# The expert stage's result stores issued by ScalarE instead of GpSimd

## The chip, the cores and the metric

The kernel runs on one core of one Trainium2 chip. The metric is the device time of one execution in microseconds (us), the median of several runs.

## The reference, cut to what matters

One inference step of a two-layer decoder for 256 prompt tokens and 8 x 4 sample tokens (288 in all, 1024 features). Each layer ends with a mixture of experts: a router picks two of 16 experts for each token, and the token's new value is a layer norm of ALPHA times its old value plus the weighted outputs of the two experts.

```python
h = jax.nn.silu(jnp.einsum('td,edf->tef', x, wg)) * jnp.einsum('td,edf->tef', x, wu)
h = h * combine[..., None].astype(h.dtype)
return jnp.einsum('tef,efd->td', h, wd)
...
xp = layer_norm(ALPHA * xp + moe(...), ln_g[l, 2], ln_b[l, 2])
```

`combine` is zero except for a token's two experts. All values are float32, and an expert has three matrices of 2 MB.

## The kernel before, in words

Attention, convolution, gating and cross-attention come first in each layer, and the change doesn't touch them. What matters is the expert stage, `experts(l)`, which runs once in each of the two layers.

**Work.** Only the tokens that chose an expert are computed for it. They are handled in chunks of at most 32 rows (CAP); an expert has one chunk, or more where it has over 32 tokens. A table of steps, computed on VectorE after the router, says which expert comes when and how many chunks it has; `last` is the number of the last chunk, read from memory by every engine. A chunk goes round the engines:

1. TensorE multiplies the chunk's rows with the gate and up matrices into `psS` (`gate_up`), and picks the rows of the next chunk into `psN` (`picked`).
2. ScalarE takes the silu of the gate half (`silu(c)`, L2158). In between it copies the next chunk's picked rows out of `psN` (`rows_in_order(c + 1)`, L2148), and after TensorE has turned them it copies them again (L2150).
3. VectorE multiplies silu and up (L1873), TensorE turns the product into `psV`, VectorE copies it (L1875) and makes the next table of rows (`table`), and TensorE multiplies with the down matrix into `psV`. Before it turns a product it waits until the last chunk's result has left `psV` (`S.y`).
4. VectorE copies the result into one half of `YS` (`rows_left`, L1881). `YS` has two halves, so chunk c waits there until the stores of chunks 0 to c - 2 have landed (`S.stored`, 64 for each chunk, from four DMAs of 16).
5. GpSimd stores the half to the HBM buffer `by_slot` with four DMAs of 32 rows x 1 KB (L2272). It waits until all earlier stores have landed before it issues the next four.

**Weights.** SyncE loads the weights of an expert with three DMAs (L682: gate and up, one run of 16 KB for each of 128 partitions; down, runs of 4 KB). There are three sets of buffers, so the load of expert step k + 3 is issued when TensorE signals that step k is done (`expert_used`). The three first experts are loaded ahead of the stage. After layer 0's experts SyncE goes on to the weights of layer 1 (L647, L658).

**End of the stage.** When the stores of all chunks but the last have landed, GpSimd gathers each token's result of the second pick (`gather(1, YB, ...)`, L2284, three indirect DMAs), then stores the last chunk, waits for it, and gathers the first pick (`gather(0, YA, ...)`). ScalarE meanwhile scales the tokens by ALPHA (L2165, L2166, `x_scaled`). VectorE adds the low pick to them (`z_low`, L1900), then the other one (`z_rows`, L1908), and takes the norm. In layer 0 TensorE then turns the rows back (L1277) and layer 1 begins; in layer 1 SyncE writes the outputs.

## Time and profile before

| | us |
|---|---|
| median of 3 runs | 1327.65 (1323.92 to 1329.11) |
| the profiled execution, its own time | 1324.23 |
| its span on the core | 1322.6 |

```profile
PE 1139.5 (86%) x10768; PEld 746.4 (56%) x10769; DVE 417.7 (32%) x1149; ACT 265.4 (20%) x541; POOL 226.4 (17%) x399
...
PE   6998788999999879998868999989998799988850
...
ACT  1013732112230321111101302111411411111101
POOL 2003995000000001322212100000000012222222
...
DMA  9746779943359729799999800715779197999972
```

The first line is each engine's busy time in the span, its share and its number of instructions. Below it the span is cut into 40 slices of 33 us; a digit is the busy share of a slice in tenths. PE is TensorE, DVE is VectorE, ACT is ScalarE, POOL is GpSimd, and DMA is the mean of the core's 16 DMA engines. Layer 0's expert stage lies in slices 15 to 22, layer 1's in the last nine. Of the page's other parts, the DMA queues are named by number: q1 is SyncE's, q10 ScalarE's (both hardware_dynamic), q0 GpSimd's (software_dynamic).

### The profile page before, as it was taken

Reading aid. Unit: us, or ns where it says so; the run is one execution under the profiler, and the core shown is the slowest. Engines: PE = TensorE matmul, PEld = TensorE weight load, DVE = VectorE, ACT = ScalarE, POOL = GpSimd, SP = SyncE. Lnnn points to the kernel's source line nnn. Section 1 sums busy time; section 2 is a strip of 40 time slices with the busy share of each in tenths; the row PEclk is TensorE's granted clock in tenths of the full one; section 3 lists DMA queues with packets and bytes.
Section 4 is the critical chain, followed back from the end, with each engine's and each line's share of the span. In section 5 each row is a group of like instructions: output and inputs, shape, how many; then the busy total and the mean of one; then the engine's idle time right before and its main releaser. Section 6 shows DMA issues by size and latency. Waiting matters only on the chain.

```text
span 1322.6 us, 27256 instructions
## 1 busy us (share of the span) xinstructions
PE 1139.5 (86%) x10768; PEld 746.4 (56%) x10769; DVE 417.7 (32%) x1149; ACT 265.4 (20%) x541; POOL 226.4 (17%) x399
## 2 busy tenths in 40 slices
PE   6998788999999879998868999989998799988850
PEld 4676545575776645554435776657765455555520
DVE  0026562713142452221112301522522622222216
ACT  1013732112230321111101302111411411111101
POOL 2003995000000001322212100000000012222222
PEclk9999997999999979998888999999999799999976
DMA  9746779943359729799999800715779197999972
GB/s 323 273 128 194 236 247 325 388 165 123 132 219 384 311 107 423 302 403 422 425 423 383 307 0 27 296 40 214 255 284 401 47 399 306 400 389 393 423 304 75
DMA packets 102625, 360.33 MB, mean 272 GB/s; under 512 B 9639, under 2 KB 11703, under 8 KB 94362
## 3 DMA queue, kind: packets, MB, share of 16 engines
q1 hardware_dynamic: 89986, 332.68, 65.7%
q0 software_dynamic: 12432, 26.51, 5.7%
q8 instruction: 42, 0.69, 0.2%
q10 hardware_dynamic: 144, 0.28, 0.1%
q14 instruction: 21, 0.17, 0.0%
HBM read 341.48 MB, written 18.38 MB: 272 GB/s over the span
## 4 chain that ended last, share of the span: by engine, by line
PE 58%; DMA 19%; DVE 10%; issue 7%; ACT 3%; SPq 1%; POOLq 1%; POOL 1%; DVEq 0%; ACTq 0%
PE acc L733 37%; DMA by_slot<-feats 10%; PE psS L733 8%; DMA ring<-in_w_exp_down 5%; PE psV L733 4%; PE psN L733 3%; DVE feats L1468 2%; DMA feats<-in_w_exp_down 2%; PE acc L1039 2%; PE acc L848 1%; DMA ring<-in_w_in_even 1%; DMA arena<-by_slot,arena 1%; PE psN L1157 1%; ACT arena L1346 1%; ACT feats L2148 1%
## 5 line engine op out<-in xcount | busy, mean ns | idle before, releaser
L733 PE MATMUL acc<-feats,ring 128*128 128x288 f32 x1280 | 315.7, 409 | 10.5 <-ACT feats L2057 4.2
L733 PEld LDWEIGHTS acc<-feats,ring 128*128 128x128 f32 x1280 | 244.7, 192 | 80.2 <-issue 9.5
L2272 POOL DMA_DIRECT2D by_slot<-feats x208 | 103.8, 499 | 524.6 <-DVE feats L1881 321.9
L733 PE MATMUL psS<-ring,feats 128*32 128x256 f32 x2176 | 138.8, 412 | 40.1 <-issue 38.8
L733 PEld LDWEIGHTS psS<-ring,feats 128*32 128x32 f32 x2176 | 74.8, 119 | 93.8 <-issue 56.0
L733 PE MATMUL psS<-arena,feats 128*32 128x256 f32 x1408 | 88.9, 402 | 22.6 <-issue 22.0
L2158 ACT ACTIVATE feats<-psS 64x256 f32<-64x256 f32 x52 | 19.6, 377 | 333.5 <-PE psS L733 333.5
L1346 ACT ACTIVATE arena<-acc 128x1024 f32<-128x1024 f32 (+6 forms) x86 | 65.4, 781 | 103.3 <-PE acc L733 34.7
L733 PE MATMUL psN<-arena,feats 128*32 128x256 f32 (+1 forms) x1360 | 83.5, 379 | 1.5 <-DVE feats L1800 1.5
L1873 DVE TENSOR_TENSOR feats<-feats,psS 64x256 f32<-64x256 f32 x52 | 22.1, 425 | 195.2 <-ACT feats L2158 194.3
L733 PEld LDWEIGHTS psS<-arena,feats 128*32 128x32 f32 x1408 | 45.7, 115 | 55.7 <-issue 31.7
L733 PE MATMUL psV<-ring,feats 128*32 128x256 f32 x1088 | 65.8, 382 | 0.8 <-DVE feats L1875 0.8
L1881 DVE COPY feats<-psV 128x256 f32 (+1 forms) x52 | 22.1, 425 | 134.9 <-DMA by_slot<-feats 95.8
L733 PEld LDWEIGHTS psN<-arena,feats 128*32 128x32 f32 x1360 | 44.1, 112 | 30.0 <-issue 3.2
L733 PE MATMUL acc<-arena,ring 128*128 128x256 f32 x256 | 58.4, 390 | 0.8 <-ACT arena L1346 0.8
L733 PE MATMUL acc<-ring,arena 128*128 128x512 f32 x128 | 56.9, 597 | 0.0
L1468 DVE SCALAR_TENSOR_TENSOR feats<-arena,cparT,feats 128x256 f32<-128x256 f32 (+1 forms) x180 | 55.9, 385 | 0.0
L733 PEld LDWEIGHTS acc<-arena,ring 128*128 128x128 f32 x256 | 49.8, 196 | 8.6 <-issue 1.5
L1628 DVE SCALAR_TENSOR_TENSOR feats<-feats,acc 128x288 f32<-128x288 f32 x32 | 14.5, 454 | 115.3 <-PE acc L733 115.3
L733 PE MATMUL acc<-arena 128*128 128x256 f32 (+6 forms) x174 | 35.5, 361 | 13.3 <-DVE arena L1434 5.7
L733 PEld LDWEIGHTS psV<-ring,feats 128*32 128x32 f32 x1088 | 31.9, 109 | 24.4 <-DVE feats L1875 6.9
L2051 ACT ACTIVATE feats<-feats 128x576 f32<-128x576 f32 x16 | 10.7, 683 | 151.5 <-DVE feats L1607 151.5
(344 smaller groups left out, 1224.3 us busy)
## 6 DMA issues: line engine op xcount, KB each, us to landing
ring<-in_w_exp_gate SPq DMA_DIRECT2D x22, 2048.0 KB, 15.1
ring<-in_w_exp_up SPq DMA_DIRECT2D x22, 2048.0 KB, 16.2
ring<-in_w_exp_down SPq DMA_DIRECT2D x22, 2048.0 KB, 24.2
arena<-in_w_exp_gate SPq DMA_DIRECT2D x10, 2048.0 KB, 15.1
arena<-in_w_exp_up SPq DMA_DIRECT2D x10, 2048.0 KB, 19.5
feats<-in_w_exp_down SPq DMA_DIRECT2D x10, 2048.0 KB, 23.8
ring<-in_cache_k SPq DMA_DIRECT2D x64, 256.0 KB, 3.2
ring<-in_cache_v SPq DMA_DIRECT2D x64, 256.0 KB, 3.1
```

Source lines behind the costliest of these rows:

```text
L733: return pe.matmul(out, lhsT, rhs, start=first, stop=last)
L848: last = pe.transpose(ACC("kt", 4 * i + b4)[:, 256 * f + P * t:256 * f + P * t + P], K[:, 2 * b4 + t, at:at + P], ident)
L1039: last = pe.transpose(ACC(f"xkt{l}", 4 * i + b4)[:, 256 * f + P * t:256 * f + P * t + P], K[:, b4, t, at:at + P], ident)
L1157: last = pe.transpose(psN[:, P * j:P * j + P], XR[:, P * j:P * j + P], ident)
L1346: return lambda out, in_: eng.activation(out, in_, ACT.Copy)
L1468: ins = dve.scalar_tensor_tensor(out=y, in0=u, scalar=tap, in1=y, op0=ALU.mult, op1=ALU.add)
L1628: dve.scalar_tensor_tensor(out=zT[:, i, :], in0=xT[:, i, :], scalar=ALPHA, in1=ACC(stage, i)[:, 0:NTOK], op0=ALU.mult, op1=ALU.add).then_i ...
L1873: dve.tensor_tensor(H[64:128, :], SG[64:128, :], psS[64:128, 0, 0:256], ALU.mult).then_inc(S.h, 1)
L1881: dve.tensor_copy(to, psV[:, 0:256]).then_inc(S.y, 1)
L2148: act.activation(XR, psN[:, 0:256], ACT.Copy).then_inc(S.rows_out, 1)
L2158: act.activation(SG[64:128, :], psS[0:64, 0, 0:256], ACT.Silu).then_inc(S.silu, 1)
L2272: pool.dma_start(by_slot[rows, 256 * q:256 * q + 256], YS[32 * q:32 * q + 32, at]).then_inc(S.stored, 16)
```

## The change

The four store DMAs of each chunk are issued by ScalarE. In its loop, pass c takes the silu of chunk c, copies the rows of chunk c + 1, waits until the stores of chunks 0 to c - 2 have landed, and then stores chunk c - 1. The last chunk is stored behind the loop, ahead of the scaling by ALPHA. GpSimd only gathers: the second pick once the stores of all chunks but the last have landed, the first pick once all have. The number and size of the DMAs, the two halves of `YS` and VectorE's waits stay as they are.

```diff
                 silu(0)
                 rows_in_order(1)
-                with act.Fori(1, last + 1) as c:
+
+                def store(c, rows, at):
+
+                    act.wait_ge(S.y, c + 2)
+                    for q in range(4):
+                        act.dma_start(by_slot[rows, 256 * q:256 * q + 256], YS[32 * q:32 * q + 32, at]).then_inc(S.stored, 16)
+
+                silu(1)
+                rows_in_order(2)
+                act.wait_ge(slots_zero, 16 * NXT)
+                store(0, slice(0, CAP), slice(0, 256))
+                with act.Fori(2, last + 1) as c:
                     silu(c)
                     rows_in_order(c + 1)
+                    act.wait_ge(S.stored, 64 * (c - 1))
+                    store(c - 1, slot_rows(c - 1), bass.ds(((c - 1) & 1) * 256, 256))
+                act.wait_ge(S.stored, 64 * last)
+                store(last, slot_rows(last), bass.ds((last & 1) * 256, 256))
...
                 last = pool.value_load(LASTI[0:1, 0:1], min_val=NE - 1, max_val=NCHUNK - 1)
-                def store(rows, at):
-
-                    for q in range(4):
-                        pool.dma_start(by_slot[rows, 256 * q:256 * q + 256], YS[32 * q:32 * q + 32, at]).then_inc(S.stored, 16)
-
-                pool.wait_ge(S.y, 2)
-                store(slice(0, CAP), slice(0, 256))
-                with pool.Fori(1, last) as c:
-                    pool.wait_ge(S.y, c + 2)
-                    pool.wait_ge(S.stored, 64 * c)
-                    store(slot_rows(c), bass.ds((c & 1) * 256, 256))
-
...
                 gather(1, YB, gathered_low)
-                pool.wait_ge(S.y, last + 2)
-                store(slot_rows(last), bass.ds((last & 1) * 256, 256))
```

## Rows read from the trace of the kernel before

**Rows 1.** Chain that ended last: start us, us, engine or DMA, what.

```profile
673.81 31.95 DMA ring<-in_w_exp_down
...
1227.92 6.92 DMA by_slot<-feats
...
1248.55 30.23 DMA ring<-in_w_exp_down
...
1294.69 1.71 DMA by_slot<-feats
...
1298.80 4.29 DMA arena<-by_slot,arena
```

**Rows 2.** Timeline of SyncE: start us, us, line, DMA issued.

```profile
577.86 0.34 SPq L682 DMA_DIRECT2D arena<-in_w_exp_gate  x1
...
1083.02 0.34 SPq L682 DMA_DIRECT2D arena<-in_w_exp_gate  x1
...
1213.87 0.35 SPq L682 DMA_DIRECT2D ring<-in_w_exp_gate  x1
```

**Rows 3.** Windows: length, busy by engine, PEclk, DMA share, GB/s.

```profile
1104.00:1114.00 10.00, 9.73 (x161) 5.55 (x160) 2.99 (x12) 1.65 (x5) 3.10 (x7) 1.00 0.31 113
...
1220.00:1240.00 20.00, 17.92 (x296) 10.25 (x298) 4.88 (x19) 2.90 (x8) 3.99 (x8) 1.00 1.02 428
```

**Rows 4.** Timeline of VectorE: start, us, instruction [idle before it <- what ended that].

```profile
1087.75 0.42 DVE L1873 TENSOR_TENSOR feats<-feats,psS 64x256 f32<-64x256 f32 x1 [4.21 <-ACT feats L2158]
...
1095.30 0.43 DVE L1873 TENSOR_TENSOR feats<-feats,psS 64x256 f32<-64x256 f32 x1 [3.16 <-ACT feats L2158]
...
1160.54 0.42 DVE L1873 TENSOR_TENSOR feats<-feats,psS 64x256 f32<-64x256 f32 x1 [1.50 <-ACT feats L2158]
...
1168.41 0.42 DVE L1881 COPY feats<-psV 128x256 f32 x1 [5.51 <-DMA by_slot<-feats]
1168.86 0.42 DVE L1873 TENSOR_TENSOR feats<-feats,psS 64x256 f32<-64x256 f32 x1
...
1218.96 0.42 DVE L1873 TENSOR_TENSOR feats<-feats,psS 64x256 f32<-64x256 f32 x1 [3.19 <-ACT feats L2158]
```

**Rows 5.** Timeline of ScalarE between two chunks of one expert.

```profile
1195.61 0.38 ACT L2150 ACTIVATE feats<-psN 128x256 f32<-128x256 f32 x1 [0.53 <-PE psN L1157]
1200.95 0.38 ACT L2158 ACTIVATE feats<-psS 64x256 f32<-64x256 f32 x1 [4.96 <-PE psS L733]
```

**Rows 6.** Timeline of GpSimd: the stores of two chunks.

```profile
1215.95 2.38 POOL L2272 DMA_DIRECT2D by_slot<-feats  x4 [3.05 <-DVE feats L1881]
1226.04 2.39 POOL L2272 DMA_DIRECT2D by_slot<-feats  x4 [7.71 <-DVE feats L1881]
```

**Rows 7.** DMA view of 1219.7 to 1225.0 us: packets by size, then by queue (packets, MB, share).

```profile
DMA packets 273, 2.24 MB, mean 424 GB/s; under 512 B 80, under 2 KB 80, under 8 KB 144
...
q0 software_dynamic: 128, 0.13, 7.0%
```

**Rows 8.** The same view of 701.9 to 703.9 us, SyncE's loads with 1 KB rows.

```profile
DMA packets 511, 0.74 MB, mean 369 GB/s; under 512 B 15, under 2 KB 436, under 8 KB 511
```

**Rows 9.** L2272, the DMA issued at 1217.8 us alone.

```profile
DMA to landing us min/median/max: 7.4/7.4/7.4
```

**Rows 10.** DMA issues on the two hardware queues: both at the start, then SyncE's L658 at 719.5.

```profile
L1957 ACTq DMA_DIRECT2D cst<-in_const x1: 435/435/435, 0.9 to 0.9; - x1
0.92 0.46 SPq L611 DMA_DIRECT2D arena<-in_x_prompt  x1
...
L658 SPq DMA_DIRECT2D ring<-in_w_in_odd x1: 5897/5897/5897, 719.5 to 719.5; - x1
```

**Rows 11.** Timeline at layer 1's end.

```profile
1289.61 1.90 ACT L2165 ACTIVATE arena<-arena 128x2048 f32<-128x2048 f32 x1
...
1292.48 5.67 DVE L1900 SCALAR_TENSOR_TENSOR arena<-arena 128x1024 f32<-128x1024 f32 x3 [0.56 <-ACT arena L2166]
...
1303.19 1.28 DVE L1908 SCALAR_TENSOR_TENSOR arena<-arena 128x1024 f32<-128x1024 f32 x1 [5.03 <-DMA arena<-by_slot,arena]
```

## The prediction

> **What bounds the kernel now.** I read the chain that ended last first. In both expert stages it ends in a long piece that is one load of down weights: 31.95 us in layer 0, landing at 705.8, and 30.23 us in layer 1, landing at 1278.8 [rows 1]. In layer 1 most of the chain ahead of it is a row of "DMA by_slot<-feats" pieces, the stores that this change moves; one stands for some 20 of them [rows 1]. Such a chain follows whatever was released last, even where it came last by 0.1 us, so it doesn't say what the stores cost. For that I went to two other views.
>
> First, SyncE's timeline against the windows. The load of step k + 3 is issued when step k is done. The issue at 1083.02 is the load behind step 2, the one at 1213.87 the load behind step 9 [rows 2]. Up to there the DMA engines run dry between loads: from 1104 to 1114 their share is 0.31 at 113 GB/s while PE is busy 9.73 of 10 us [rows 3]. So in that stretch the pace of the chunks decides when the next load starts. Behind 1213.87 four loads (steps 12 to 15) run without a gap, at share 1.02 and 428 GB/s [rows 3], until 1278.8: 64.9 us, 16.2 each, whatever the chunks do. **The end of layer 1's stage is therefore: time at which step 9 is done, plus four loads, plus one chunk and the tail.** In layer 0 the same point is the issue at 577.86, behind step 5 [rows 2], with eight loads to 705.8, 16.0 us each.
>
> Second, VectorE's timeline, for the pace. Within one expert two L1873 lie 7.55 us apart (1087.75, 1095.30); this is TensorE's own time for a chunk. Later in layer 1 VectorE waits for a landing 5.51 us before its result copy, and the next L1873 comes at 8.32 us instead (1160.54 to 1168.86) [rows 4]. From 1087.75 to 1218.96 there are 16 steps, 131.2 us, 9 of them within an expert [rows 4]. Four of the nine are late like the one shown (0.66 to 0.79 us, 2.9 together), and about 0.5 of that is made good at the change of expert behind them. So **all of the store waits cost about 2.4 us in layer 1's paced stretch**, and that is the whole prize. In layer 0's paced stretch I found no L1873 that was late.
>
> **Removed from GpSimd.** Its issues, 2.38 us for four [rows 6], were beside other work; removing their busy time (103.8 us on the page) is worth nothing by itself.
>
> **Added to ScalarE.** Four hardware-queue issues per chunk. ScalarE's only DMA took 0.435 us [rows 10], SyncE's with register addresses 0.34 [rows 2] and a move each; 4 x 0.45 = 1.8 us. They start when the rows of the next chunk are copied, and until the next silu ScalarE is idle 4.96 us within an expert [rows 5]. So the issue itself is hidden, with 3.2 us to spare; uncovered it would be 1.8 us x 52.
>
> **The wait that is new** is the one ahead of the issue: the stores of chunk c - 2 must have landed before ScalarE issues those of c - 1. What is queued behind it on ScalarE is silu(c + 1), and for that wait VectorE, then TensorE. Before, the same wait stood on GpSimd, behind which nothing else was queued. There a late store delayed only the result copy two chunks later, which can itself be 3 us late (TensorE needs the copy only when it turns the next product). Now the chain from store to store must fit in 7.55 us, or 10.7 once, with the 3.2 spare used up.
>
> **How long is that chain?** Under weight traffic GpSimd's was 10.1 us from store to store (1215.95 to 1226.04) [rows 6]. The DMA issued last, at 1217.8, took 7.4 us to land, at 1225.2 [rows 9]. The packets of this store lie in the window of 5.3 us: 128 of its queue, 8 on each of 16 engines, and 129 (273 less 144) weight packets of over 8 KB [rows 7]. So each engine took store and weight packets in turn, one for one, and a turn lasted 5.3 / 8 = 0.66 us. GpSimd's 8 packets per engine are 4 of data, two rows of 1 KB together (0.13 MB in 64), and 4 for the semaphore. SyncE's queue doesn't put rows together: where it loads 1 KB rows, 436 of 511 packets are under 2 KB [rows 8]. If ScalarE's queue is like SyncE's, a store has 8 data and 4 semaphore packets per engine, 12 turns, 7.9 us in place of 5.3. With the rest as it was (3.8 us from issue to first packet, 0.2 to the landing) the chain is 11.9 us. The bounds: 6.5 us, if ScalarE's packets are built like GpSimd's and start 1.2 us after the issue, as an idle landing of 1.71 us [rows 1] suggests; and 12.5 us, if each turn is a little longer. I take 11.9, since packet form is the thing that the rows show for the kind of queue. In the down phase, a third of a load, the weight packets are of 4 KB and the chain is about 6 us.
>
> The Trainium skill, "DMA: Bandwidth & Descriptors", SWDGE vs HWDGE, calls the hardware path the faster one, with 0.6 us to the first byte against 1 us for GpSimd's. By it the chain would be 9.7 us, not 11.9, and the first term below nothing. The rows show no store on a hardware queue under load.
>
> **Sum, layer 1.** 11.9 us is 1.2 over the 10.7 that can be hidden. One gate-and-up phase (two thirds of 16.2 us) holds one such store, and four experts of the paced stretch have three or four chunks, where the 7.55 us spacing holds: 4 x 1.2 = 4.8. Across a change of expert the spacing is a us wider, and I count nothing. The old 2.4 us go. Net +2.4; bounds -2.4 (short chain) and, with the chain limiting every chunk, far above (first rival).
> **Layer 0.** Up to step 5 two experts have three or four chunks: 2 x 1.2 = +2.4; bounds 0 and +8.
> **Tails.** In layer 1 ScalarE is done with its row copies at 1289.6 [rows 11]. Then: stores of the last but one chunk 1.8, landing of the last of these 1.7 - 0.45 later, 1292.7; stores of the last chunk to 1294.5, landed about 1295.8, against 1294.69 + 1.71 = 1296.4 before [rows 1]. The second pick's gather, done early before, now starts at 1293.2 and issues until 1297; the first pick's follows at 1297.7 and lands after 4.29 us [rows 1] or a little later behind it in the queue, at 1302 to 1303. The ALPHA scaling, before from 1289.61 under the wait, comes behind the stores: 2.9 us to 1297.5. z_low takes 5.67 us [rows 11], so z_rows starts at 1303.2 or 1303.6, against 1303.19 [rows 11]: +0.3, bounds -0.5 and +4. Layer 0's tail has the same shape in front of more loads, and the gather was the last thing there too: 0, bounds -1 and +4.
>
> Sum 2.4 + 2.4 + 0.3 = **+5.1 us**: 1329.3 against the profiled execution's own 1324.23. That execution is 3.4 us below the median of the runs, so against the median it is 1332.8.
>
> **The rivals.**
> *The chain paces every chunk* (slower). The forecast counts on dry stretches between loads, in which the chain catches up. Without them a load's 16.2 us hold 10.8 / 11.9 + 5.4 / 6 = 1.8 stores, 9.0 us each, and silus go at that pace. The 16 steps of layer 1 would take 144 in place of 131.2 [rows 4], +13; in layer 0 the 8 chunks of steps 3 to 5 would take 72 in place of about 64 up to 577.86 [rows 2], +8. With +0.3 that is 1349. It decides once the mean chain is over the mean step, 131.2 / 16 = 8.2 us. Against it: share 0.31 between loads [rows 3] shows stretches in which a store is quick.
> *Short chain* (no loss). ScalarE's stores start sooner or are packed: -2.4 in layer 1, 0 in layer 0, +0.3: 1325.6. For it speaks the idle landing of 1.71 us [rows 1]; against it rows 7 and 8 together.
> *A shared generator.* SyncE's L658 at 719.5 was held 5.9 us in its issue, and the next one 7.8 [rows 10], because its queue was full. If ScalarE's issue waits for SyncE's, the last store of layer 0, due at 720.8, is held until 725 or 733, and the first pick with it: +5 to +11 on top of the forecast, 1341. Against it: at the start ScalarE and SyncE issued at the same moment and took 0.435 and 0.46 us [rows 10], neither twice as long.
> The Trainium skill, "Perfetto Trace Analysis", DMA Instruction — HWDGE, has the generator locked for one queue at a time. The 0.9 us row does not look like it, the 719.5 row can't tell.
> *The change does nothing that shows*, because loads end the stage either way, is the lower half of the forecast's range.
>
> **How the numbers follow.** Forecast 0.50 (1327 to 1339), pacing chain 0.17, short chain 0.19, shared generator 0.14. A measurement of this kernel tells about 0.5%, 6.6 us, from no change. The forecast is slower by over that in 0.3 of its cases (0.15); the two slow rivals nearly always (0.30); the short chain gives a gain over 6.6 us only if the tails gain as well (0.05). So slower 0.45, faster 0.05, same 0.50. The range goes from the short chain's lower side, 1322, to just over the pacing chain, 1350.
>
> **What the profile after would show.** Right: ScalarE's queue with about 52 x 192 = 9984 packets of its own; a store-to-store chain of 11 to 12 us in gate-and-up phases; some silus up to 1 or 2 us late; the issue behind step 9 at 1214 to 1220; four loads of 16 us behind it; z_rows no more than 1 us later after the last chunk. Wrong: 128 packets per store (short chain); silu intervals of 10 us through an expert (pacing chain); ScalarE issues of several us beside L658 (shared generator). The number falls if the loads themselves take another time than 16 us.

## The result, and the profile after

The changed kernel takes **1357.87 us** (median of 6 runs, 1351.26 to 1359.52), the kernel before 1325.28 us (6 runs, 1323.92 to 1329.11; the first three of them had the median 1327.65 from which the forecast starts). The ratio is 1.0228, with a 95% interval of 1.0209 to 1.0248. The forecast was 1332.8 with a range of 1322 to 1350. So the change costs 32.6 us, and the forecast saw 5.

The page of the changed kernel: the span, TensorE's line, the queues of GpSimd (q0) and ScalarE (q10) with packets, MB and share, and the second line of the chain that ended last.

```profile
span 1356.3 us, 27154 instructions
PE 1153.8 (85%) x10768; PEld 756.7 (56%) x10769; DVE 417.8 (31%) x1149; ACT 265.2 (20%) x541; POOL 126.6 (9%) x191
...
q0 software_dynamic: 5776, 19.68, 4.1%
q10 hardware_dynamic: 10128, 7.11, 1.7%
...
PE acc L733 36%; DMA by_slot<-feats 15%; PE psS L733 7%; DMA ring<-in_w_exp_down 4%; ACTq L2167 4%; PE psV L733 3%; PE psN L733 3%; DVE feats L1468 2%; PE acc L1039 2%; PE acc L848 1%; DMA ring<-in_w_in_even 1%; DMA arena<-by_slot,arena 1%;
```

GpSimd is busy 100 us less and nothing is gained by it. ScalarE's queue has 10128 packets; less the 144 that it had before, that is 9984, or 192 for each of 52 stores, as forecast. The stores' share of the chain went from 10% to 15%, and their issues (ACTq L2167) are now in it with 4%. A piece of 6.92 us stood for that stretch before [rows 1]; one of the pieces in layer 1 now, from the chain in order of time:

```profile
1186.86 9.04 DMA by_slot<-feats
```

**Where the 33.7 us between the two spans lie.** I read three instructions in each layer's stage from VectorE's timelines: the first L1873, the last result copy (L1881) and the first z_rows (L1908). The differences add up.

| us | before | after | difference |
|---|---|---|---|
| start to layer 0's first L1873 | 485.31 | 486.46 | +1.2 |
| layer 0's stage, to its last result copy | 233.41 | 239.52 | **+6.1** |
| tail of layer 0, from there to z_rows | 16.46 | 23.22 | **+6.8** |
| z_rows to layer 1's first L1873 | 319.57 | 326.95 | **+7.4** |
| layer 1's stage | 236.75 | 247.48 | **+10.7** |
| tail of layer 1 | 11.69 | 13.25 | +1.6 |
| z_rows to the end | 19.41 | 19.42 | 0.0 |

Over the kernels below, the first stretch, whose code none of them changes, lies between 481.7 and 489.8 us, so 4 us either way there mean nothing. The stretch from z_rows to layer 1's first L1873 must be read with the same care: in the kernels below it takes 322.6 to 326.9 us, also where nothing near it was changed, and the 319.6 of the kernel before is the lowest of all. The table compares one execution with one other, so some of its +7.4 may be the luck of the execution that was profiled. The expectations below that give layer 0's tail as 20.0 us before and 27.2 after, and the stages' losses as 5.7 and 10.7, count from and to the last L1873 instead of the last result copy. That was a poor choice: the last L1873 can come before the last down weights have landed, and then the tail holds a wait for a load. I give the results from the last result copy.

**The stages.** ScalarE's timeline in layer 1 under weight traffic (start, us, instruction, idle before and what ended it), then TensorE's, then windows (busy by engine PE, PEld, DVE, ACT, POOL; granted clock; DMA share; GB/s).

```profile
1185.32 1.86 ACTq L2167 DMA_DIRECT2D by_slot<-feats  x4
1187.53 0.38 ACT L2158 ACTIVATE feats<-psS 64x256 f32<-64x256 f32 x1 [8.07 <-issue]
...
1196.22 1.86 ACTq L2167 DMA_DIRECT2D by_slot<-feats  x4
1198.43 0.38 ACT L2158 ACTIVATE feats<-psS 64x256 f32<-64x256 f32 x1 [8.94 <-issue]
```

```profile
1189.24 1.93 PE L733 MATMUL psV<-ring,feats 128*32 128x256 f32 x32 [0.17 <-DVE feats L1875]
...
1199.32 0.69 PE L1175 MATMUL psV<-cst,feats 128*128 128x128 f32 x2 [3.40 <-DVE feats L1873]
...
1200.39 3.64 PE L733 MATMUL psV<-ring,feats 128*32 128x256 f32 x32
```

```profile
1180.00:1200.00 20.00, 13.89 (x237) 8.25 (x226) 2.76 (x9) 1.90 (x5) 0.00 (x0) 0.97 1.01 421
1200.00:1210.00 10.00, 9.95 (x125) 4.66 (x123) 1.92 (x8) 1.10 (x3) 0.00 (x0) 0.72 0.56 221
```

(The four issues of a store are one row, x4.) They take 1.86 us, and the next four come 10.9 us after them; the silu stands right behind each, "issue" being the wait for the stores that the profile files under ScalarE's queue. Before, the silu followed TensorE [rows 5]. The two silus are 10.9 us apart, two L1873 within one expert were 7.55 [rows 4]. TensorE, busy 13.89 of 20 us here against 17.92 in a loaded window of before [rows 3], loses 3.40 us to one late silu. And then something that I had not priced: the same 32 products that took 1.93 us take 3.64 behind that pause, and the granted clock of the next window is 0.72. So a pause costs its length and then a stretch at the lower of the two levels, 1.2 instead of 2.4 GHz. Over the whole paced stretch, from the load behind step 2 to the one behind step 9, the windows read, before and after:

```profile
1084.00:1214.00 130.00, 119.56 (x1998) 68.50 (x1986) 30.16 (x111) 18.31 (x48) 29.88 (x60) 1.00 0.92 375
```

```profile
1104.00:1246.00 142.00, 122.98 (x2004) 69.94 (x1999) 30.51 (x112) 18.27 (x48) 0.00 (x0) 0.98 0.86 348
```

TensorE needs 3.4 us more for as many products, which is about what a mean clock of 0.98 gives: an estimate of 0.02 x 142 = 2.8 us. The other 7 to 8 of the 10.4 us are idle time.

The same stretch between SyncE's issues takes 141.2 us instead of 130.8, and layer 0's 70.2 instead of 63.7 [rows 2]. Of the 17 distances between ScalarE's stores in layer 1's stretch, six are 10.5 to 12.4 us; of the 16 between GpSimd's stores before, one is 11.9 us and no other over 10.2. Of the 17 silus there, seven were released by a store (its wait or its issue) and ten by TensorE. From the issue behind step 9 to the last result copy layer 1 takes 78.0 us instead of 77.6.

**The tail of layer 0**, changed kernel: ScalarE, GpSimd, VectorE, TensorE.

```profile
721.60 0.38 ACT L2158 ACTIVATE feats<-psS 64x256 f32<-64x256 f32 x1 [13.73 <-PE psS L733]
...
724.34 7.78 ACTq L2167 DMA_DIRECT2D by_slot<-feats  x8
732.16 1.91 ACT L2180 ACTIVATE arena<-arena 128x2048 f32<-128x2048 f32 x1 [7.97 <-issue]
...
730.38 1.07 POOL L2287 DMA_INDIRECT arena<-by_slot,arena  x1 [0.29 <-POOL arena L2291]
...
738.61 2.61 POOL L2287 DMA_INDIRECT arena<-by_slot,arena  x1 [0.27 <-POOL arena L2295]
...
725.98 0.42 DVE L1881 COPY feats<-psV 128x256 f32 x1 [1.63 <-PE psV L733]
738.36 2.02 DVE L1900 SCALAR_TENSOR_TENSOR arena<-arena 128x1024 f32<-128x1024 f32 x1 [11.95 <-DMA arena<-by_slot,arena]
...
749.20 1.28 DVE L1908 SCALAR_TENSOR_TENSOR arena<-arena 128x1024 f32<-128x1024 f32 x1 [4.51 <-DMA arena<-by_slot,arena]
...
757.17 0.30 PE L1277 MATMUL acc<-cst,arena 128*128 128x128 f32 x1 [3.74 <-ACT arena L2062]
759.93 0.47 PE L1277 MATMUL acc<-cst,arena 128*128 128x128 f32 x1 [2.46 <-ACT arena L2062]
761.07 6.33 PE L1277 MATMUL acc<-cst,arena 32*128 32x32 f32 x22 [0.66 <-ACT arena L2062]
```

The kernel before at the same place:

```profile
703.93 2.39 POOL L2272 DMA_DIRECT2D by_slot<-feats  x4 [12.43 <-issue]
...
720.03 2.38 POOL L2272 DMA_DIRECT2D by_slot<-feats  x4 [5.31 <-DVE feats L1881]
...
727.62 1.03 POOL L2284 DMA_INDIRECT arena<-by_slot,arena  x1 [0.52 <-POOL arena L2294]
...
714.73 0.38 ACT L2158 ACTIVATE feats<-psS 64x256 f32<-64x256 f32 x1 [14.42 <-PE psS L733]
...
719.69 5.85 DVE L1900 SCALAR_TENSOR_TENSOR arena<-arena 128x1024 f32<-128x1024 f32 x3 [0.55 <-ACT arena L2166]
...
735.18 1.28 DVE L1908 SCALAR_TENSOR_TENSOR arena<-arena 128x1024 f32<-128x1024 f32 x1 [9.64 <-DMA arena<-by_slot,arena]
...
747.05 4.04 PE L1277 MATMUL acc<-cst,arena 32*128 32x32 f32 x22 [0.66 <-ACT arena L2062]
```

Most of this comes from the order of the program. The last chunk's silu waits 14 us for its weights in both kernels. GpSimd stored the chunk before it at 703.93, in front of that silu at 714.73, and issued the second pick's gather from 711.20. ScalarE has the same store behind the silu in its program, so it goes out at 724.34, and the gather, the last store (held until the first has landed), the scaling and z_low come one after another from there. TensorE has some 28 us of layer 1's key and value products to do in that time. Already before, they ended too early, and TensorE stood 0.66 us; now it stands 3.74 + 2.46 + 0.66 us, and its clock falls (below).

### The profile page after: what moved, and what is told of

Its sections match the earlier page's. It is cut to its first block, busy times and chain, and to the rows that moved or that the text cites. A ratio compares the mean times of both kernels' runs of the same rounds, so it can differ in the third digit from the quotient of the medians.

```text
span 1356.3 us, 27154 instructions
## 1 busy us (share of the span) xinstructions
PE 1153.8 (85%) x10768; PEld 756.7 (56%) x10769; DVE 417.8 (31%) x1149; ACT 265.2 (20%) x541; POOL 126.6 (9%) x191
## 3 DMA queue, kind: packets, MB, share of 16 engines
q10 hardware_dynamic: 10128, 7.11, 1.7%
## 4 chain that ended last, share of the span: by engine, by line
PE 55%; DMA 22%; DVE 10%; issue 4%; ACTq 4%; ACT 3%; SPq 1%; POOL 0%; DVEq 0%; POOLq 0%
PE acc L733 36%; DMA by_slot<-feats 15%; PE psS L733 7%; DMA ring<-in_w_exp_down 4%; ACTq L2167 4%; PE psV L733 3%; PE psN L733 3%; DVE feats L1468 2%; PE acc L1039 2%; PE acc L848 1%; DMA ring<-in_w_in_even 1%; DMA arena<-by_slot,arena 1%; ACT arena L1346 1%; PE psN L1157 1%; DVE arena L1911 1%
## 5 line engine op out<-in xcount | busy, mean ns | idle before, releaser
L733 PE MATMUL acc<-feats,ring 128*128 128x288 f32 x1280 | 320.2, 414 | 11.4 <-DMA ring<-in_w_in_even 4.5
L733 PEld LDWEIGHTS acc<-feats,ring 128*128 128x128 f32 x1280 | 247.8, 194 | 82.4 <-issue 10.4
L1873 DVE TENSOR_TENSOR feats<-feats,psS 64x256 f32<-64x256 f32 x52 | 22.1, 425 | 200.7 <-ACT feats L2158 200.0
L733 PE MATMUL psV<-ring,feats 128*32 128x256 f32 x1088 | 70.8, 404 | 1.7 <-DVE feats L1875 1.7
L1881 DVE COPY feats<-psV 128x256 f32 (+1 forms) x52 | 22.1, 424 | 148.9 <-DMA by_slot<-feats 107.0
L1175 PE MATMUL psV<-cst,feats 128*128 128x128 f32 x104 | 23.3, 306 | 29.7 <-DVE feats L1873 29.7
## 6 DMA issues: line engine op xcount, KB each, us to landing
ring<-in_w_exp_up SPq DMA_DIRECT2D x22, 2048.0 KB, 17.6
```

The source lines that it names most:

```text
L733: return pe.matmul(out, lhsT, rhs, start=first, stop=last)
L1175: last = pe.transpose(psV[:, P * j:P * j + P], H[:, P * j:P * j + P], ident)
L1873: dve.tensor_tensor(H[64:128, :], SG[64:128, :], psS[64:128, 0, 0:256], ALU.mult).then_inc(S.h, 1)
L1881: dve.tensor_copy(to, psV[:, 0:256]).then_inc(S.y, 1)
```

## The experiments

Ratios are against the kernel before, run on the same chip in the same minutes, with 95% intervals. A *turn* is one packet of a store and the weight packet that a DMA engine moves beside it; the *chain* is what lies between two stores: the issues, the first packet, the turns and the landing. Stages and tails are read from one profiled execution of each kernel.

**1. The changed kernel, gate and up loaded with runs of 4 KB.** Four DMAs for each matrix, so that a weight packet is a quarter as large (the counts of the waits on a load go with it and are not shown). Everything else is that of the changed kernel.

```diff
-sp.dma_start(where.rearrange("p (k n) -> p k n", k=(8, 8, 4)[j]),
-             w[l, bass.ds(e, 1)].rearrange(runs, p=P)).then_inc(landed, 16)
+for i in range(PARTS[j]):          # PARTS = (4, 4, 1)
+    r = slice((8, 8, 4)[j] // PARTS[j] * i, (8, 8, 4)[j] // PARTS[j] * (i + 1))
+    sp.dma_start(where.rearrange("p (k n) -> p k n", k=(8, 8, 4)[j])[:, r],
+                 w[l, bass.ds(e, 1)].rearrange(runs, p=P)[:, r]).then_inc(landed, 16)
```

> The changed kernel, but each gate and each up matrix is loaded by four DMAs with runs of 4 KB instead of one with 16 KB; nothing else. Turn theory (a store packet waits for one weight packet, so its burst goes by the size of that packet): a store's burst falls from 7.5 us to 3 or less, the chain from store to store from 11 to under 7.5, no silu waits for a landing in the paced stretches, and the 6.5 and 10.7 us that the two stages lost come back; the tail of layer 0 stays long: ratio to before 1.008 to 1.013. Issue theory (the four issues and the hardware queue's own latency cost the time, not the neighbours): bursts stay over 6 us, ratio 1.020 to 1.025.

Measured: 1333.9 us, ratio 1.007 (1.0045 to 1.0095), just under the range. 24 of the 32.6 us are gone. The stages take 234.1 and 235.3 us, as before the change, and that is 17.6 us of the 24 in the two profiled executions; 4.8 more lie in the first stretch, which none of these kernels changes. The tail of layer 0 stays at 23.4. DMA view of both kernels under gate-and-up traffic, first the changed kernel from a store's first packet to its landing (1188.6 to 1196.2), then this one from 1185 to 1190:

```profile
DMA packets 489, 3.34 MB, mean 440 GB/s; under 512 B 96, under 2 KB 224, under 8 KB 316
...
q10 hardware_dynamic: 192, 0.13, 5.3%
```

```profile
DMA packets 620, 2.07 MB, mean 414 GB/s; under 512 B 64, under 2 KB 131, under 8 KB 620
...
q10 hardware_dynamic: 115, 0.07, 4.4%
...
by_slot<-feats ACTq DMA_DIRECT2D x4, 32.0 KB, 2.6
```

In the first, the store's 192 packets, 12 for each of 16 engines, need 7.6 us, 0.63 us for each of the 12, beside 489 - 316 = 173 weight packets of over 8 KB: nearly one for one, at the turn forecast. (124 smaller packets of SyncE's lie in the window too.) In the second the weight packets are under 8 KB and a store's DMA lands in 2.6 us (median), where the four of the changed kernel at 1185.3 to 1186.9 took 6.8.

**2. The kernel before with the same runs of 4 KB.** The same edit.

> The kernel before with the same 4 KB runs for gate and up. Turn theory: GpSimd's chain falls from 10.1 us to about 6, the late L1873 of layer 1 vanish, gain 2 to 3 us: ratio 0.997 to 1.000. If 4 KB packets cost the loads bandwidth, a load takes over 16.2 us and the ratio is over 1.00 (17 us a load would be +10 us, 1.007).

Measured: 1327.57 us, ratio 1.0007 (0.9982 to 1.0032). Layer 1's stage is 1.9 us shorter, near the 2.4 us that the store waits cost before, but layer 0's is 2.9 us longer, and no gain can be measured in the whole. So the 24 us of run 1 aren't a gain of small runs as such; they are what small runs do to a store on the changed path.

**3. The changed kernel with runs of 8 KB.** `PARTS = (2, 2, 1)`.

> The changed kernel with the gate and up loads as two DMAs each, runs of 8 KB instead of 16 KB; the tail is left as it is. Turn theory: a turn with an 8 KB packet takes about half of 0.66 us, 12 turns 4 us, the chain from store to store about 8 us under load, near the mean step of 8.2: most of the stage losses go, stages within 2.5 us of those of before, 1334 to 1338 as with 4 KB. If a store has to wait for whole loads or for a number of packets instead of for their bytes, 8 KB brings half of the gain of 4 KB or less, 1344 or more.

Measured: 1331.04 us, 1.0028 (1.0004 to 1.0053), stages 232.1 and 234.3, tail of layer 0 23.6. Half the packet brings all that a quarter brings, as the turn theory said, and the time is a little below its range. So the loss isn't proportional to the turn. Runs 1 to 3 agree with a loss that starts where the chain from store to store no longer fits.

**4. One DMA for a store.** 128 rows into a buffer of its own, 9 packets for each engine.

```diff
-for q in range(4):
-    act.dma_start(by_slot[rows, 256 * q:256 * q + 256], YS[32 * q:32 * q + 32, at]).then_inc(S.stored, 16)
+act.dma_start(by_part[rows], YS[:, at]).then_inc(S.stored, 16)
```

> The changed kernel with one DMA per chunk instead of four, 128 rows of 1 KB into a buffer of its own laid out by chunk. Left out: the rows don't get into the buffer from which the gathers read, so the gathers fetch zeros and the tokens' new values lack the experts' part. Each of 16 DMA engines then has 8 data packets and 1 semaphore packet for a store, 9 turns instead of 12, and ScalarE issues 0.4 us instead of 1.9. Turn theory: 3 turns of 0.66 us and 1.5 us of issue fewer, store to store 10.9 - 3.5 = 7.4 us under load; both stage losses (5.7 and 10.7 us) vanish, tail of layer 0 shortens by some 3 us: 1330 to 1336. If the number of packets were not what counts (only bytes or the start of a hardware DMA), the chain would shorten by the issue alone and half of the stage losses stay: 1343 to 1350.

Measured: 1339.34 us, 1.0084 (1.0048 to 1.0119), above the 1330 to 1336 of the turn theory and below the other range. Layer 0's stage takes 230.1 us, the whole loss there is gone. Layer 1 can't be compared, because without the experts' part its tokens choose otherwise and it has 29 chunks instead of 27; its L1873 lie 7.5 to 9.0 us apart in the paced stretch, as before. The weight packets stayed at 16 KB, so fewer turns help as shorter ones do. But this kernel also issues in 0.35 us what took 1.9, so it can't tell turns from issues; runs 1 and 3, which keep the issues, do that.

**5. The kernel before with four packets more per store and engine.** Two small DMAs more on GpSimd for each chunk, to a buffer that nobody reads; the chain waits for them too.

```diff
+for q in range(2):
+    pool.dma_start(aside[16 * q:16 * q + 16], YS[32 * q:32 * q + 16, at]).then_inc(S.stored, 16)
```

> The kernel before with two more DMAs of 16 rows x 1 KB per chunk on GpSimd, into a buffer that nobody reads: 12 packets per engine for a chunk in place of 8, as ScalarE's queue has, but the wait on GpSimd. Turn theory in its plain form (chain length sets the pace wherever the wait stands): chain 12 us in gate and up phases, VectorE's result copies late, stages +6 and +10 as in the changed kernel, ratio 1.010 to 1.016. Place theory (the same chain costs only where a silu is queued behind the wait): ratio 1.000 to 1.005, since a result copy may be late by 3 us and a store by 7.5 before TensorE waits.

Measured: 1373.94 us, 1.0358 (1.0308 to 1.0409). Distances between stores rise to 13.1 us at the most, 9.7 in the mean of layer 1's paced stretch, the stages to 243.3 and 251.1 (+9.8 and +14.4), the tails to 30.0 and 17.5 us (+13.5 and +5.8). The time is above both ranges: I had thought of neither the tails nor the 1 us that the two issues add to each chain. A long chain on GpSimd, with nothing queued behind it but stores, costs as much in the stages as the somewhat shorter one on ScalarE, or more. My theory of the place, that it is the silu behind the wait that makes the loss, falls in this form.

**6. The kernel before with ScalarE waiting as well.** GpSimd stores; ScalarE only has the wait.

```diff
 with act.Fori(2, last + 1) as c:
     silu(c)
     rows_in_order(c + 1)
+    act.wait_ge(S.stored, 64 * (c - 1))
```

> The kernel before with one wait added: ScalarE, behind the rows of chunk c + 1, waits until the stores of chunks 0 to c - 2 have landed, as in the changed kernel, while GpSimd still issues the stores. Place theory (the wait in front of the next silu is what costs): the stages grow as in the changed kernel, +5.7 and +10.7 us, so 1342 or more. Length theory (only the chain from store to store costs, wherever the wait stands): GpSimd's chain of 10.1 us under load fits as before, both stages stay within 2 us of before, 1326 to 1329. The tails should stay within 1 us under both.

Measured: 1327.74 us, 1.0015 (0.9987 to 1.0044), stages 233.5 and 237.4. The wait in front of the silu alone costs nothing that can be measured, because GpSimd's chain of 8 turns fits under it. With runs 1 to 5: **the stages lose by the length of the chain, which 12 turns in place of 8 bring about.** Whether the place adds something at equal length isn't shown, because the chain of run 5 is longer than the changed kernel's.

**7. The last chunk's store on GpSimd again.** The changed kernel, with GpSimd storing the last chunk behind the second pick's gather; ScalarE scales at once.

```diff
-act.wait_ge(S.stored, 64 * last)
-store(last, slot_rows(last), bass.ds((last & 1) * 256, 256))
...
 gather(1, YB, gathered_low)
+pool.wait_ge(S.y, last + 2)
+for q in range(4):
+    pool.dma_start(by_slot[slot_rows(last), 256 * q:256 * q + 256], 
+                   YS[32 * q:32 * q + 32, bass.ds((last & 1) * 256, 256)]).then_inc(S.last, 16)
...
```

> The changed kernel, but the last chunk of each layer is stored by GpSimd behind its first gather, and ScalarE goes straight on to the scaling by ALPHA; all other stores stay with ScalarE. If the tails cost what the trace shows (7.2 us to z_rows in layer 0, some 4.6 us more on a TensorE that had gone idle, 1.6 in layer 1), ratio 1.010 to 1.015. But the stores of the last chunk but one are still ScalarE's and still late, so the second pick's gather stays late: if that is what the tail cost, the ratio stays at 1.018 to 1.023.

Measured: 1367.31 us, 1.0293 (1.0247 to 1.0339), 9 us more than the changed kernel. The tail of layer 0 became 26.9 us, that of layer 1 17.0. A miss on both theories, and its trace gave the next one: the last store now goes out at 734.69, behind a gather that itself waits for the late store of the chunk before. Put behind that gather, the last store can only go out later.

**8. The last but one chunk's store ahead of the last silu.** The second loop only waits: its last pass is the wait for the stores of chunks 0 to last - 2.

```diff
-with act.Fori(2, last + 1) as c:
+with act.Fori(2, last) as c:
     silu(c)
     rows_in_order(c + 1)
     act.wait_ge(S.stored, 64 * (c - 1))
     store(c - 1, slot_rows(c - 1), bass.ds(((c - 1) & 1) * 256, 256))
+with act.Fori(NE - 1, last + 1) as c:
+    act.wait_ge(S.stored, 64 * (c - 1))
+store(last - 1, slot_rows(last - 1), bass.ds(((last - 1) & 1) * 256, 256))
+silu(last)
+rows_in_order(last + 1)
```

> The changed kernel with the store of the last but one chunk issued ahead of the last chunk's silu instead of behind it (a short loop of waits stands for the wait on the earlier stores). In layer 0 the last silu waits for its weights until 721.6, while the result of the chunk before it is ready at about 704. Order theory: the store, and the second pick's gather with it, come 18 us earlier, the last store goes out as soon as its result is there, the tail of layer 0 falls from 27.2 us to 20 to 23, and the 4.6 us that TensorE loses behind it go as well; the stages keep their +5.7 and +10.7: 1345 to 1350. If instead the landing of the last stores beside the next loads, or ScalarE's late ALPHA scaling, makes the tail long, it stays over 25 us and the time within 3 us of 1358.

Measured: 1351.07 us, 1.0183 (1.0136 to 1.023), 1 us over the range. GpSimd and VectorE in this kernel:

```profile
724.81 1.07 POOL L2292 DMA_INDIRECT arena<-by_slot,arena  x1 [0.29 <-POOL arena L2296]
...
739.98 2.44 POOL L2292 DMA_INDIRECT arena<-by_slot,arena  x1 [0.27 <-POOL arena L2300]
...
737.63 5.85 DVE L1900 SCALAR_TENSOR_TENSOR arena<-arena 128x1024 f32<-128x1024 f32 x3 [6.16 <-ACT arena L2186]
749.13 1.28 DVE L1908 SCALAR_TENSOR_TENSOR arena<-arena 128x1024 f32<-128x1024 f32 x1 [5.66 <-DMA arena<-by_slot,arena]
```

The last result copy is at 731.04. The gather comes 6 us ahead of it instead of 4 us behind it, z_low no longer waits for it but for the scaling, and the tail falls from 23.2 to 18.1 us. The stages keep their loss (241.2 and 247.1). The order theory holds for 5 of the 6.8 us. (Counted as the expectation counts it, from 27.2 to 23.7.) What I expected beside it did not come: TensorE still waits 1.27 + 0.80 us, and still has its half clock.

**9. The last store not held for the one ahead of it.** A semaphore of its own in place of `act.wait_ge(S.stored, 64 * last)`.

> The changed kernel with a semaphore of its own for the last chunk's store, so that it isn't held until the last but one has landed (that wait lasted from 726.2 to 729.8 in the changed kernel). Order theory (the late second pick's gather and the scaling behind 8 stores make the tail): the last store goes out 3.8 us earlier, the scaling too, but the second pick's gather isn't earlier, because the last but one chunk's store is still behind the last silu; z_low still starts when that gather has landed, about 12 us behind the last result copy; tail of layer 0 23.2 -> 20 to 22, time 1354 to 1357. Landing theory (the last store's own landing is what z_rows waits for): the tail loses all 3.8 us and TensorE's idle time behind it with them, 1350 to 1353.

Measured: 1348.9 us, 1.0174 (1.0148 to 1.0201), tail 18.7 us. It gains more than both theories said, some 2 us of it in layer 1's stage (245.4 us), where nothing was changed. z_low starts 12.6 us behind the last result copy, as the order theory has it; but the first pick's gather is issued before z_low runs, and its three issues take 0.96, 0.95 and 0.86 us. In the changed kernel they run beside z_low and take 2.61, 2.09 and 1.52. I had not counted that term at all. So the tail has a second remedy, nearly as good as the first and in another place (23.2 to 18.7 us here, to 18.1 in run 8): the runs show a row of late steps, each of which can be shortened, and not one step that is the cause.

**10. The kernel before with only the last store on ScalarE**, ahead of the scaling. `gather(1)` stays early.

> The kernel before with only the last chunk's store moved to ScalarE, ahead of its ALPHA scaling, on a semaphore of its own; the last but one chunk's store and the second pick's gather stay early on GpSimd. Order theory: the tails stay near 20.0 and 15.7 us, up to 2 us longer in layer 0 for a landing of 12 packets beside 16 KB and 2 KB packets instead of 8, because the ALPHA scaling ends only at about 725: 1326 to 1331. Landing theory (a hardware store beside the next layer's loads lands so late that the first pick's gather starts late): tail of layer 0 25 us or more, and TensorE idle behind it, 1335 or more.

Measured: 1328.61 us, 1.0033 (1.0006 to 1.006), tail 19.3 us (16.5 before), 25.9 counted as the expectation counts it. By the tail's length the landing theory had it right (25 or more), by the time the order theory. The trace shows why the tail is longer: scaling and z_low come later, z_low at 724.05 instead of 719.69, so that it meets the gather's issues.

**11. Both remedies**, runs of 4 KB and the early store.

> The changed kernel with both remedies at once: the gate and up matrices loaded with runs of 4 KB instead of 16 KB, and the last but one chunk's store ahead of the last silu. If the two causes found (turns with 16 KB packets in the stages, program order in the tail) are the whole of the loss and independent, their single gains of 24 us and 7 us add up: 1358 - 31 = 1327, within 0.3% of before, with layer 0's tail at 17 to 19 us from the last result copy to z_rows and the stages at 233 to 236 us. If something else in the move costs time (ALPHA scaling behind the stores, four waits more on ScalarE), 4 us or more are left over: 1331 and above.

Measured: 1333.66 us, 1.0071 (1.0042 to 1.01). Stages 235.7 and 236.6, tail 17.1: all near where they should be, and yet 8 us are left, as much as with the first remedy alone. So the gains don't add up, and I looked for a third term behind the tail: from z_rows to the last gelu of layer 1's first product it takes 51.6 us in this kernel, 51.8 in the changed one, 47.2 in the kernel before. Windows of 4 us at that place, the kernel before and then the one with both remedies:

```profile
752.00:756.00 4.00, 4.00 (x19) 3.11 (x18) 0.00 (x0) 1.44 (x2) 1.29 (x2) 1.00 0.56 212
```

```profile
749.00:753.00 4.00, 1.21 (x6) 0.47 (x4) 1.46 (x8) 3.02 (x4) 2.15 (x3) 1.00 1.06 388
753.00:757.00 4.00, 4.00 (x17) 2.24 (x15) 1.62 (x3) 1.38 (x4) 0.00 (x0) 0.55 1.04 352
757.00:761.00 4.00, 4.00 (x11) 2.50 (x11) 0.58 (x1) 2.30 (x3) 0.66 (x1) 0.50 0.83 301
761.00:765.00 4.00, 4.00 (x13) 2.96 (x12) 0.00 (x0) 0.00 (x0) 0.79 (x2) 0.67 0.01 3
```

TensorE is busy 1.21 of 4 us, and then gets 0.55, 0.50 and 0.67 of its clock for 12 us. Those three windows do at most (0.55 + 0.50 + 0.67) x 4 = 6.9 us' worth of work in 12. The kernel before pauses 0.66 us there and keeps 1.00. In all these kernels the last turning of rows (L1277) starts 11.9 us behind z_rows, with the pause and without (747.05 - 735.18 before, 761.07 - 749.20 in the changed kernel). So behind z_rows it is the lower clock alone that costs the 4.4 to 4.6 us; the pause itself is the late z_rows seen from TensorE.

Two rows warn against giving these us to the change. Run 6 left the tail as it was (16.8 us) and paused 0.42 us, and took 50.3 us for this stretch; run 10 took 51.6. Both are within 0.4% of the kernel before. Of all the kernels only that of run 2 kept the full clock there as the kernel before did (47.2 us). So this term is seen in the traces, but one profiled execution each doesn't show how much of the remaining 8 us it is.

**12. Both remedies, and the ALPHA scaling ahead of the last store**, in the time in which ScalarE waits for the last result.

```diff
 silu(last)
 rows_in_order(last + 1)
+act.activation(XTOK[:, 0:2, :], XTOK[:, 0:2, :], ACT.Copy, scale=ALPHA)
+act.activation(XTOK[0:32, 2, :], XTOK[0:32, 2, :], ACT.Copy, scale=ALPHA).then_inc(x_scaled, 1)
 act.wait_ge(S.stored, 64 * last)
 store(last, slot_rows(last), bass.ds((last & 1) * 256, 256))
```

> The changed kernel with the 4 KB runs and the early store as in the last kernel of that kind, and the ALPHA scaling moved ahead of the last chunk's store, into the 4 us in which ScalarE waits for the last result. Clock theory (the 8 us that the kernel with both remedies still loses are TensorE's 2.8 us of idle time ahead of layer 1's first products and the fall to half clock for some 10 us behind it): z_low starts right behind the last result copy and is over before the first pick's gather is issued, the gather's issues take 1.0 us each again, tail of layer 0 16 to 16.8 us, TensorE idle under 1 us, granted clock 1.00 behind it (or a short piece of 0.5 to 0.75 at most): 1326 to 1330. If the rest is something else, z_rows comes earlier but the time stays 1332 to 1335.

Measured: 1329.82 us, 1.0019 (0.9994 to 1.0044): no difference from the kernel before that can be measured. Windows behind the tail:

```profile
745.00:749.00 4.00, 1.98 (x9) 0.79 (x7) 1.45 (x8) 3.05 (x4) 2.15 (x3) 1.00 1.05 386
749.00:753.00 4.00, 4.00 (x18) 2.33 (x18) 1.45 (x4) 1.78 (x3) 0.00 (x0) 0.63 1.05 351
753.00:757.00 4.00, 4.00 (x10) 2.74 (x11) 0.54 (x1) 1.88 (x2) 0.84 (x1) 0.52 1.03 376
```

The time came out in the range of the clock theory, but not by its path. z_low waits for the second pick's gather until 722.52, the first pick's first issue still meets it and takes 2.44 us, the tail is 18.1 us and not 16 to 16.8, and TensorE pauses 2.0 us. The lower clock lasts 8 us instead of 12, 2.9 us in place of 4.4 up to that gelu. From the last result copy to that gelu the two kernels take 68.7 and 68.1 us: where the edit works, it brings 0.6 us. The rest of the difference between their profiled executions lies in the first stretch (3.0 us) and in the stages (2.1 and 1.8), which the edit doesn't touch. So the clock theory isn't shown by this run, and what made the last 3.8 us is open. No version here beats the kernel before by a measurable amount.

## Why the prediction was wrong

**What bounds the kernel: right.** Up to the load behind step 9 the chunks' pace sets the loads. The whole loss of layer 1's stage stands ahead of that load (+10.4 of 10.7 us), and the four loads behind it take their time.

**Removing GpSimd's work: right.** 100 us of busy time less gained nothing.

**The issues and their packets: right.** 1.86 us for four against 1.8; 12 packets per engine against 8; turns of 0.63 against 0.66 us; store to store 10.9 in the pair shown against 11.9, and up to 12.4 at the most. The short chain fell, and with it the 9.7 us that stood beside it, which the prediction doesn't work out. The Trainium skill's sentence on the faster hardware path ("DMA: Bandwidth & Descriptors", SWDGE vs HWDGE) did not decide here. At their quickest, ScalarE's stores land 0.2 us sooner than GpSimd's (1.5 against 1.7 us from issue to landing), and under load four packets more for each engine are, by an estimate, 4 x 0.63 = 2.5 us.

**The sum over the stages: the step that failed.** I let each expert with three or four chunks meet one long store, 1.2 us over what can be hidden, and wrote "4 x 1.2 = 4.8" for layer 1 and "2 x 1.2" for layer 0. Measured: six long distances in layer 1's paced stretch, and +10.7 and +6.1 us for the stages. Two things were wrong in the term. The 3.2 us of ScalarE's spare time can be used once: behind a chain of 12.4 us comes another of 10.9 (ScalarE at 1185.32 and 1196.22), which finds nothing spare, and then costs the full distance to 7.55 us. And TensorE's pauses cost granted clock as well, some 3 of the 10.4 us in layer 1, which I had at nothing. The rival "the chain paces every chunk" comes nearest in time: it gave 144 and 72 us for the two paced stretches, and they took 141.2 and 70.2. Its mechanism happened in part: seven of the 17 silus were released by a store. Whether its condition, a mean chain over 8.2 us, was met isn't shown. The mean distance between stores is 8.9 us, against 8.4 before, but a distance between stores is the pace of the chunks, whoever sets it. The row that I set against it, share 0.31 between loads [rows 3], was one window of 10 us picked where the DMA engines were dry; the share over the whole paced stretch was 0.92, and that window I did not read. I also had the 2.4 us of the old waits go; the waits of L1881 on stores grew from 95.8 to 107.0 us.

**Layer 0's tail: the second step that failed.** The prediction's "the same shape in front of more loads" and a 0 stood for +6.8 us, with bounds of -1 and +4. In layer 1 I followed the moved store through ScalarE's program and got +0.3, measured +1.6, within the bounds. In layer 0 I only said that it is alike. It isn't: there the next layer's loads run, so the last stores land after 5.4 to 6.3 us instead of 1.7 [rows 1], the first pick's gather meets z_low, and TensorE's cover of 28 us was already used up, by 0.66 us. My bound of +4 asked what could be late and not how much cover was left under it.

**From z_rows to layer 1's stage: not in the sum at all.** +7.4 us, of which 4.6 up to that gelu are the lower clock. How much of it belongs to the change is open: 3.1 of the 4.6 also stand in run 6, whose tail and time are those of the kernel before, and in the kernel before with 4 KB runs, which kept the full clock, the stretch took 326.85 us too.

**The shared generator: it did not show.** That SyncE's queue was full at 719.5 was my reading; the rows show only how long the issue lasted. In the changed kernel SyncE's issue of L658 was held while ScalarE issued beside it. The third of these three began at 726.8 and was held 4.09 us; ScalarE's began at 730.2:

```profile
L658 SPq DMA_DIRECT2D ring<-in_w_in_odd x3: 367/582/4092, 725.7 to 726.8; - x3
```

```profile
L2167 ACTq DMA_DIRECT2D by_slot<-feats x3: 327/328/328, 730.2 to 731.2; - x3
```

The first of ScalarE's falls into SyncE's 726.8 to 730.9 and took no longer than the others. Here the two queues did not hold each other up in their issue, and the trace speaks against a lock held over the whole of a stalled issue.

## What to carry to other kernels

When small stores share the DMA engines with large loads, count the store's packets per engine and multiply by the time of a neighbour's packet; the kind of queue changes that count, and smaller loads shorten the turn. Judge whether that chain can catch up from the DMA share of the whole stretch, not of the best window in it, and let slack be used only once. When an issue moves to another engine, write down what stands ahead of it in that engine's program at every stage end, and how many us of cover are left under each wait that it feeds: a tail whose cover is used up already has no room for anything. And profile more than one execution before a term of a few us is given to a change.

## What the runs showed of the hardware that I had not expected

**A pause of TensorE can be paid for twice.** In the stage shown above it cost 3.40 us, and then 3.64 us instead of 1.93 for 32 products. In runs 8, 11 and 12 and in the changed kernel, behind 2 to 7 us of idle time with little work between, the granted clock was 0.50 to 0.67 for 8 to 12 us; the lower of its levels is 1.2 GHz, the upper 2.4. The length of the pause alone doesn't decide it: one of 0.66 us left it at 1.00 in the kernel before, one of 0.42 us in the kernel of run 6 was followed by 0.74 and then this window:

```profile
753.00:757.00 4.00, 4.00 (x9) 2.86 (x10) 0.00 (x0) 1.70 (x2) 1.32 (x2) 0.50 0.42 160
```

**Packets differ by queue.** ScalarE's hardware queue sends one packet for each row of 1 KB, GpSimd's software queue puts two rows together: 192 and 128 for the same 0.13 MB with its semaphores.

**GpSimd's indirect issue took 2.5 times as long beside z_low**, 2.61 against 1.03 us, and a plain TENSOR_TENSOR of one element, 0.18 us otherwise, took 2.00 us on GpSimd in run 10 while z_low ran.
